# Sixteen products of constants on TensorE at six places of a two-block forward pass

## The reference

```python
mod = (silu(c) @ ada_w + ada_b).reshape(B, 6, D)          # shift, scale, gate twice
h = rmsnorm(x, norm_mix_g) * (1 + scale_m) + shift_m
x = x + gate_m * token_mix(h, ...)                        # GLA, latent attention, merge, w_out
h = rmsnorm(x, norm_ffn_g) * (1 + scale_f) + shift_f
x = x + gate_f * swiglu(h, ffn_w_in, ffn_w_down)
x = rmsnorm(x, final_norm_g)
for l in range(2):                                        # second block, two layers
    h = rms_norm(x, pre_norm_g[l])
    mixed = [retention | diff attention | rg_lru](h @ w_in[l])
    x = x + rms_norm(mixed @ w_out[l], post_norm_g[l])
```

## Time and profile before

| | |
|---|---|
| median of 3 runs | 2704.96 us (2703.41 to 2705.41) |
| profiled execution, its own time | 2703.97 us |
| its span | 2701.9 us |
| mean granted clock of TensorE | 0.992 |
| busy: PE, DVE, ACT | 2581.1, 1758.6, 1304.1 us |
| moved | 554.27 MB, mean 205 GB/s |

### The profile page before, as it was taken

One profiled execution on the slowest core, in us unless ns is written; L12 is line 12 of the kernel. 1 busy time (PEld: TensorE's weight loads), 2 busy tenths in 40 slices (PEclk: granted clock), 3 DMA queues, 4 the chain that ended last, 5 costly groups with the idle time before them and its releaser, 6 DMA issues.

```text
span 2701.9 us, 35639 instructions
## 1 busy us (share of the span) xinstructions
PE 2581.1 (96%) x12959; PEld 2177.9 (81%) x12959; DVE 1758.6 (65%) x2452; ACT 1304.1 (48%) x1897; POOL 73.3 (3%) x110
## 2 busy tenths in 40 slices
PE   2889999999999999999999999999999999999999
PEld 2778887888878787888888888889887887978886
DVE  5787786777677765677655555566656655565664
ACT  2434455444555444544443444455655545565553
POOL 0000000000000000000000000002000101100000
PEclk9899999999999999999999999999999999999999
DMA  9885666888666666678766666566555464655464
GB/s 332 282 274 174 186 185 180 287 301 277 213 214 220 210 202 204 193 252 262 246 200 193 190 186 186 183 188 184 157 182 172 133 217 135 179 171 180 139 204 133
DMA packets 341449, 554.27 MB, mean 205 GB/s; under 512 B 24463, under 2 KB 135805, under 8 KB 340637
## 3 DMA queue, kind: packets, MB, share of 16 engines
q1 hardware_dynamic: 335488, 541.79, 63.7%
q0 software_dynamic: 3168, 7.12, 0.8%
q10 hardware_dynamic: 2620, 3.09, 0.3%
HBM read 549.83 MB, written 2.10 MB: 204 GB/s over the span
## 4 chain that ended last, share of the span: by engine, by line
PE 83%; issue 5%; DVE 4%; ACT 3%; DMA 0%; POOL 0%; DVEq 0%; POOLq 0%; ACTq 0%
PE gp L809 76%; PE tp L809 6%; PE tp L812 2%; ACT whi L1231 1%; DVE wlo L1842 1%; DVE acc L1848 1%; DMA raw<-in_ffn_w_in_dram 0%; ACT L1231 0%; DVE xs L1842 0%; DVE yd L1842 0%; ACT hraw L1231 0%; DVE ul L1842 0%; ACT sx L1231 0%; ACT mxh L1231 0%; ACT lxt L1231 0%
## 5 line engine op out<-in xcount | busy, mean ns | idle before, releaser
L1842 DVE TENSOR_TENSOR wlo<-raw,whi 128x1024 fp32r<-128x1024 f32 (+1 forms) x830 | 983.3, 1197 | 616.6 <-ACT whi L1231 613.9
L1231 ACT ACTIVATE whi<-raw 128x1024 fp32r<-128x1024 f32 (+1 forms) x830 | 849.1, 1036 | 617.7 <-PE gp L809 492.3
L809 PE MATMUL gp<-whi,h 128*128 128x512 f32 (+1 forms) x2944 | 927.4, 387 | 4.6 <-DVE wlo L1842 3.0
L809 PEld LDWEIGHTS gp<-whi,h 128*128 128x128 f32 x2944 | 551.4, 188 | 109.7 <-issue 11.9
L809 PE MATMUL gp<-h,whi 128*128 128x512 f32 (+1 forms) x1936 | 603.9, 371 | 30.6 <-DVE wlo L1842 20.1
L809 PE MATMUL gp<-wlo,h 128*128 128x512 f32 (+1 forms) x1472 | 561.0, 381 | 0.0
L809 PE MATMUL gp<-h,wlo 128*128 128x256 f32 x1680 | 474.1, 282 | 0.0
L809 PEld LDWEIGHTS gp<-h,whi 128*128 128x128 f32 x1936 | 352.8, 192 | 101.2 <-issue 32.6
L809 PEld LDWEIGHTS gp<-h,wlo 128*128 128x128 f32 x1680 | 320.6, 191 | 1.1 <-issue 1.0
L809 PEld LDWEIGHTS gp<-wlo,h 128*128 128x128 f32 x1472 | 277.9, 189 | 45.2 <-issue 1.2
L1848 DVE SCALAR_TENSOR_TENSOR acc<-raw,cact,acc 128x512 f32<-128x512 f32 x298 | 223.3, 749 | 11.4 <-DMA raw<-in_ada_w_dram 4.9
(11 more groups left out here) (329 smaller groups left out, 2643.6 us busy)
## 6 DMA issues: line engine op xcount, KB each, us to landing
raw<-in_w_in_dram SPq DMA_DIRECT2D x310, 512.0 KB, 4.4
raw<-in_ffn_w_in_dram SPq DMA_DIRECT2D x176, 512.0 KB, 4.6
raw<-in_ada_w_dram SPq DMA_DIRECT2D x158, 512.0 KB, 4.9
raw<-in_w_out_dram SPq DMA_DIRECT2D x96, 512.0 KB, 4.3
raw<-in_ffn_w_down_dram SPq DMA_DIRECT2D x88, 512.0 KB, 4.3
raw<-in_w_in_dram SPq DMA_DIRECT2D x64, 384.0 KB, 3.5
raw_first<-in_ada_w_dram SPq DMA_DIRECT2D x34, 512.0 KB, 5.4
raw<-in_gla_wo_dram SPq DMA_DIRECT2D x32, 512.0 KB, 5.4
```

Source lines behind the costliest of these rows:

```text
L809: return e.matmul(o, l, r, start=start, stop=stop)
L1231: return e.activation(o, i, f, **kw)
L1842: return e.tensor_tensor(o, a, b, op)
```

## The change

A new part `warm` issues sixteen plain float32 products of constants: the identity as stationary operand, the identity and a block of ones (256 columns) as moving operand, all into one `tp` bank, which nobody reads. It is added to `fnorm` for each j, to `ffn` and to the end of the first layer.

```diff
@@ stage_steps, kind == "fnorm" (j = 0 to 3)
-        return [step(("fn_T", (2 * j,), 1), ("fn_T", (2 * j + 1,), 1), need=[("start",)]),
+        return [step(("fn_T", (2 * j,), 1), ("fn_T", (2 * j + 1,), 1), ("warm", ("h", j), 1), need=[("start",)]),
@@ kind == "ffn"
-            first = [("f_rn", (), 0), *[("f_sc", (n,), 0) for n in range(4)]] if pair == 0 else []
+            first = [("f_rn", (), 0), ("warm", ("hf",), 1), *[("f_sc", (n,), 0) for n in range(4)]] if pair == 0 else []
@@ kind == "lend", l == 0
-            a = [("le_rn", (l,), 0), ("le_add", (l, 0), 0)] if j == 0 else []
+            a = [("le_rn", (l,), 0), ("warm", ("h1",), 1), ("le_add", (l, 0), 0)] if j == 0 else []
@@ pe_program
+        def warm(us, *at_stage):
+
+            (u,) = us
+            bk = empty(u)
+            for n in range(16):
+                last = mm(bk[:, 0:S], ident, cst[:, C_ID:C_ID + S], True, True)
+            last.then_inc(tp_full[u.b], 1)
@@ the table of TensorE's parts
-        parts = dict(rows=rows, ada_mod=ada_mod, ...
+        parts = dict(rows=rows, warm=warm, ada_mod=ada_mod, ...
```

More of the change, by code:

```diff
@@ L1211, in unit @@
             last.then_inc(mm_done, 1)
-        parts = dict(rows=rows, ada_mod=ada_mod, ada_out=ada_out, fn_T=fn_T, gk_la=gk_la, gk_kr=gk_kr, gk_krt=gk_krt,
+        parts = dict(rows=rows, warm=warm, ada_mod=ada_mod, ada_out=ada_out, fn_T=fn_T, gk_la=gk_la, gk_kr=gk_kr, gk_krt=gk_krt,
                      gla_sum=gla_sum, gla_sc=gla_sc, gla_av=gla_av, gla_og=gla_og, lat_T=lat_T, pr_qn=pr_qn, pr_kn=pr_kn, pr_rr=pr_rr, pr_sc=pr_sc,
```

## The result

The changed kernel takes 2724.56 us (median of 4, 2723.91 to 2726.16) against 2704.81 before (median of 4): ratio 1.0074, 95% interval 1.0060 to 1.0088. In another set of executions (median 2724.88) it stood at 1.0075 (1.0061 to 1.0089). It is slower by 19.8 us, where 14.9 were predicted. The profiled execution, 2726.16 us, is the slowest of the four, so the lateness read from its trace, 22.5 us, is more than the 19.8 of the medians.

The account below looks back on a forecast made before the run. TensorE was taken as the bound nearly everywhere (83% of the chain). 0 + 6.5 + 2.9 + 6.4 + 0.4 - 1.3 = +14.9 us on the profiled 2703.97 gives 2718.9, as median 2719.9; range 2711 to 2725.

Parts of the forecast that it names:

- The length of a group: At all six places: sixteen products, two records each, take 6.5 us at 2.4 GHz, 0.404 us a product.
- the rival of one record a product: All six places: one pass a product, sixteen take 3.2 us, +3.3 in all, 2708 us; chance 0.06.
- The prediction's other figure: From the Trainium skill: 262 cycles, 0.109 us a product and 1.7 us for sixteen, making the places nearly free.
- First quarter: Wait until 58.93: products end 1.5 us late, but `ada_mod` waits for VectorE's `acc`: 0; bounds -1.1 and +1.5.
- Second quarter: Products ahead of ready `v` push back ScalarE's `h` and the chain, no restart saved: +6.5; bounds +4.8 and +8.
- Third quarter: Products ahead of ready `v`; ScalarE's idle time absorbs 3.5 of 6.5 us: +2.9; bounds +0.8 and +5.
- Fourth quarter: No wait from 213.16 on, so the group adds to TensorE's own order: +6.4; bounds +3.2 and +7.
- The low bound of half: Fourth quarter: +3.2 us if half the group is taken up by waits of the stages behind.
- Feed-forward norm: Turning starts 0.8 us late but at full clock, no restart saved that counts: +0.4; bounds 0 and +0.9.
- Second layer: Turning starts 1.5 us late, but 12 records take 2.7 instead of 5.3 us: -1.3; bounds -2.0 and +1.5.
- the clock that pays: Early shifts are caught up, restarts at 58.93, 106.59, 162.07 and 2263.68 saved: -7.6 us, 2697; chance 0.05.

Follow-up runs that it names:

- the kernel cut to the waits: Against the kernel before: 16 and 17 products behind `v` (second, third quarter), 12 at the norm, 11 at the second layer, none elsewhere: 2698.72 us, ratio 0.9981.

## Why the prediction was right, step by step

The direction and the mechanism held, and the range too, but only just and with some luck: 2724.56 lies inside 2711 to 2725, and two of the four executions (2725.06 and 2726.16) don't. The forecast, +14.9 against +19.8, was 4.9 us low, and this is where:

- **The length of a group.** Predicted 6.5 us, 0.404 a product from the gates' rows; measured 6.91, 0.432. The structure, two records a product, was right, and with it the rival of one record a product fell. The step that was mis-sized is the division: the next product started 0.03 us behind the start of the 14th record, so the 2.83 us hold 13 gaps, not 14. The same row has the right pace in its second number: 3.18 less one record's own 0.38 is 2.80 for 13 gaps, 0.215 a record or 0.431 a product. Three groups on the path: 1.2 us. The prediction's other figure, 0.109 us a product, is a quarter of what was measured.
- **First quarter.** Predicted 0, measured +0.5 alone (ratio 0.9993 to 1.0011) and +1.5 in the first profile. The step that held is that the saved restart is worth nothing, because `acc` is awaited at 67.2; what it lacked is the fall of the clock behind that wait, for which it had no term.
- **Second quarter.** Predicted +6.5; measured +6.5 to +6.9 against four traces without the group and +8.8 against two, +5.7 by the times of that group alone. The prediction took the half-clock stretch over `v` for a fixed part of the stretch; it was absent in two of six kernels without the group. ScalarE's `h` behind the reading of `v`, the wait unchanged at 7.4, and no restart saved: all as written.
- **Third quarter.** Predicted +2.9; +2.7 in the trace of that group alone, +3.5 by its times, +5.0 in the first profile of the change, where 3 us of half clock fell inside the group. The 3.5 us of ScalarE's idle time absorbed what they should; TensorE's wait was predicted 4.3 and was 4.21.
- **Fourth quarter.** Predicted +6.4; measured +6.91, the group's length again. The low bound of half had nothing to it.
- **Feed-forward norm.** Predicted +0.4, measured +0.74, the same in every profile with sixteen products there: the group is 0.4 us longer than the 6.5 of the sum.
- **Second layer.** Predicted -1.3, measured -0.4 on average of profiles, -1.0 against the one trace that the prediction had. The stretch of half clock that it meant to save was the longest of five.
- **What has no term.** About 1.5 us for each half-clock stretch of some 3 us that falls where TensorE has work. Both profiles of the changed kernel have five of them, the profile of before one; but the kernels with one group have three or four, most of them far from their group, and the kernel cut to the waits has two. So the profile of before, on which the sum rests, had few by chance, and that the groups make them more frequent is likely only at 68. With the fall at 68 (1.5) and the length (1.2) some 2 us of the 4.9 stay open.

Of the rivals, the clock that pays had the wrong sign for this change and the right idea for another place: by the Trainium skill (TensorE: Matmul & The Clock Gate, section Why this matters for your kernels) no long idle gap should stand between bursts of matmuls. The traces agree where the gap was filled and only there: with it filled, TensorE took 11.6 us from the wait of the second quarter to the next sums, else 13.3 to 14.0.

## What to carry to other kernels

In this kernel products that only keep TensorE busy were free in a wait and cost their full length a few instructions away from it: before placing them, look not at how long the engine waits at a border but at which instruction the bracket stands, and what ready work and whose queue lie ahead of it. Then cut the group to the wait, since an overhang of 2 us eats what a restart gives back, and leave out the places where another engine's work is due next anyway. Read the length of such an operation from the starts inside its row, not from its first start to the next instruction's, and expect the gain to be small: four well cut groups won 0.2%.

## What the runs showed of the hardware

- A plain float32 product with 128 stationary and 256 moving columns runs as two records and takes 0.432 us at 2.4 GHz back to back (32 records in 6.91 us). At 1.2 GHz it takes twice that: in the changed kernel's third quarter the row of 32 records was 8.76 us instead of 7.07, with the granted clock at 0.50 over 157 to 160 and at 0.80 over 160 to 161, so that 3.4 us at half clock lost 1.7.
- The clock falls to 1.2 GHz for some 3 us also behind short waits, in some executions and not in others of the same instructions. Behind the sums of the second quarter, ahead of which TensorE waited 2.25 us in all thirteen profiles, it fell in ten; behind those of the third, with waits of 1.03 to 1.06 us, in seven; behind the next ones, with 0.96 to 1.01, in four. Each fall costs about 1.5 us where TensorE has work. A trace of one execution is uncertain by that much at each border, which only several profiles showed.
- Up to about 64 us most of these traces give the granted clock as 1.00, also where records run at half pace (11 weight records in 2 us over 60 to 62 before, 19 in the changed kernel). There the pace has to be read from the records.
